# One of the two convolved chunks moves from TensorE to GpSimd, the squares of the head norms from GpSimd to ScalarE

## The reference

```python
def even_mixer(h, w_in, w_out, conv_w, conv_b, ln_g, ln_b, q_g, k_g, sinks):
    proj = h @ w_in
    a_val, a_gate, q, k, v = jnp.split(proj, cuts, axis=-1)      # 512, 512, 512, 128, 128 channels
    u = a_val * jax.nn.sigmoid(a_gate)
    u = lax.conv_general_dilated(u, conv_w[:, None, :], (1,), ((CONV_WIDTH - 1, 0),), ...,
                                 feature_group_count=CONV_CH) + conv_b     # 31 taps, one filter a channel
    u = jax.nn.silu(layer_norm(u, ln_g, ln_b))
    q = rms_norm_2(q.reshape(b, s, SWA_KV_HEADS, SWA_GROUP, HEAD_DIM), q_g)   # 8 heads of 64
    k = rms_norm_2(k.reshape(b, s, SWA_KV_HEADS, HEAD_DIM), k_g)              # 2 heads of 64
    o, _, _ = banded_attention(q, k, v, SWA_WINDOW - 1, sinks)                # causal, 128 positions back
    return jnp.concatenate([u, o.reshape(b, s, -1)], axis=-1) @ w_out
```

## Time and profile before

| | before |
|---|---|
| median of 3 runs | 1739.1 us (1738.5 to 1739.69) |
| the profiled execution | 1739.11 us |
| its span in the trace | 1737.3 us |
| PE busy | 96% |
| DVE busy | 70% |
| ACT busy | 54% |
| POOL busy | 29% |
| the even mixer, first input unit to last output unit | about 938 to 1077 us |

### The profile page before, as it was taken

How to read it: one execution, slowest core, us unless ns; L and a number is a source line. 1 busy time by engine, 2 the same in 40 slices (tenths; PEclk the granted TensorE clock), 3 DMA queues, 4 the chain that set the end, 5 groups by cost and what they waited for, 6 DMA issues and landing times. The chain is left out here.

```text
span 1737.3 us, 30201 instructions
## 1 busy us (share of the span) xinstructions
PE 1663.6 (96%) x10274; PEld 1452.1 (84%) x10274; DVE 1212.2 (70%) x2026; ACT 940.8 (54%) x1549; POOL 510.7 (29%) x492
## 2 busy tenths in 40 slices
PE   7896999999997999999999998999999999899999
PEld 6785899988876999888889867888888889678888
DVE  5776777756776777667765956777577765867763
ACT  5454566534553666456645655665376644456652
POOL 0040433310222434234421004443144411444430
PEclk9998999999998999999999998999999999999999
DMA  7330465654322566556665303656556655246662
GB/s 255 99 120 25 126 189 181 220 174 146 104 80 62 169 182 206 193 169 186 201 201 156 118 16 110 193 183 218 163 176 190 208 185 166 86 122 188 186 219 96
DMA packets 70494, 272.09 MB, mean 157 GB/s; under 512 B 7824, under 2 KB 8976, under 8 KB 70416
## 3 DMA queue, kind: packets, MB, share of 16 engines
q1 hardware_dynamic: 70416, 271.07, 49.6%
HBM read 269.99 MB, written 1.05 MB: 156 GB/s over the span
## 5 line engine op out<-in xcount | busy, mean ns | idle before, releaser
L828 DVE TENSOR_TENSOR wl<-raw,wh 128x1024 fp32r<-128x1024 f32 (+1 forms) x470 | 619.5, 1318 | 127.4 <-ACT wh L536 121.5
L536 ACT ACTIVATE wh<-raw 128x1024 fp32r<-128x1024 f32 (+1 forms) x470 | 525.9, 1119 | 218.5 <-PE gb L1275 115.9
L1271 PE MATMUL gb<-hx,wh 128*128 128x512 f32 x1512 | 543.9, 399 | 0.0
L1272 PE MATMUL gb<-hx,wl 128*128 128x256 f32 x1512 | 424.9, 281 | 0.0
L1271 PE MATMUL gb<-gux,wh 128*128 128x512 f32 x960 | 341.3, 395 | 0.0
L1271 PEld LDWEIGHTS gb<-hx,wh 128*128 128x128 f32 x1512 | 284.8, 188 | 59.2
L1258 PE MATMUL gb<-hx,wh 128*128 128x256 f32 x1008 | 298.6, 296 | 18.3 <-DVE hx L845 10.1
L1272 PEld LDWEIGHTS gb<-hx,wl 128*128 128x128 f32 x1512 | 286.4, 189 | 7.6
L1259 PE MATMUL gb<-hx,wh 128*128 128x256 f32 x1008 | 287.9, 286 | 0.0
L1260 PE MATMUL gb<-hx,wl 128*128 128x256 f32 x1008 | 287.4, 285 | 0.0
L1272 PE MATMUL gb<-gux,wl 128*128 128x256 f32 x960 | 268.5, 280 | 0.0
(11 more groups left out here) (213 smaller groups left out, 2051.7 us busy)
## 6 DMA issues: line engine op xcount, KB each, us to landing
raw<-in_wa SPq DMA_DIRECT2D x374, 512.0 KB, 3.6
raw<-in_wb SPq DMA_DIRECT2D x96, 704.0 KB, 4.2
x<-in_x SPq DMA_DIRECT2D x2, 512.0 KB, 6.1
out_x<-x SPq DMA_DIRECT2D x8, 128.0 KB, 3.1
row<-in_row SPq DMA_DIRECT2D x1, 836.0 KB, 11.4
tab<-in_bias SPq DMA_DIRECT2D x3, 256.0 KB, 4.4
con<-in_const SPq DMA_DIRECT2D x1, 544.0 KB, 8.5
tab<-in_bias SPq DMA_DIRECT2D x1, 512.0 KB, 5.4
```

The lines of the kernel that those rows point to most:

```text
L536: nc.scalar.activation(wh[:, slot, 0:nt * P], raw[:, slot, 0:nt * P], ACT.Copy).then_inc(s_hi, 1)
L828: nc.vector.tensor_tensor(wl[:, slot, 0:nt * P], raw[:, slot, 0:nt * P], wh[:, slot, 0:nt * P].bitcast(f32), ALU.subtract).then_inc(s_lo, 1)
L1271: nc.tensor.matmul(bank[:, :], a, both(k), start=start and k == 0, stop=False)
L1272: nc.tensor.matmul(bank[:, 0:SEQ], b, high(k), start=False, stop=False)
```

## The change

Three things, all in the even mixer:

- Chunk 3 is no longer convolved on PE. The table loses its "diag" 4 to 7 and "taps" 4 to 7 (ACT's 31 diagonals and PE's 31 products) and gains one entry, "pconv", at unit 7 behind the second "operand". On POOL it is a new function, `convolve`: 31 products of the shifted operand with one tap, broadcast along the row, and 30 additions into `yc(6)`, 61 `tensor_tensor` instructions of 128x256. The products rotate through three parts of `kkf`, so that the product of tap k is issued ahead of the addition of tap k-1. An instruction waits for all but the one just issued.
- "convolved" 1 on ACT waits for POOL instead of PE's taps and reads `yc(6)` instead of PSUM. Its place in ACT's queue is the same.
- The three squares of the head norms are an ACT instruction (Square) at the same places of the table.

```diff
-               "even": "sigmoids diagonals operands ...
+               "even": "pool_convolved sigmoids diagonals operands ...
...
-                      (5, "conv", 3), (6, "taps", 1), (6, "conv", 8), (7, "sig", 3), (7, "taps", 2), (7, "operand", 1),
-                      (7, "conv", 9), (8, "taps", 3), (8, "conv", 10), (8, "diag", 4), (9, "turn", 0), (9, "convolved", 0),
+                      (5, "conv", 3), (6, "taps", 1), (6, "conv", 8), (7, "sig", 3), (7, "taps", 2), (7, "operand", 1), (7, "pconv", 0),
+                      (7, "conv", 9), (8, "taps", 3), (8, "conv", 10), (9, "turn", 0), (9, "convolved", 0),
...
+            def convolve(m):
+                src, prods = operand[1], [kkf[:, k * SEQ:(k + 1) * SEQ] for k in range(3)]
...
+                def product(k):
+                    tap = PRM["ecw"] + 31 * 3 + k
+                    step(nc.gpsimd.tensor_tensor(yc(6) if k == 0 else prods[k % 3], src[:, k:k + SEQ],
+                                                 view(prm[:, tap:tap + 1], [[0, SEQ]]), ALU.mult))
+                pool.wait_ge(m["operands"], 2)
+                product(0)
+                product(1)
+                for k in range(2, 31):
+                    pool.wait_ge(s_pch, steps[0] - 1)
+                    product(k)
+                    pool.wait_ge(s_pch, steps[0] - 1)
+                    step(nc.gpsimd.tensor_tensor(yc(6), yc(6), prods[(k - 1) % 3], ALU.add))
+                pool.wait_ge(s_pch, steps[0])
+                nc.gpsimd.tensor_tensor(yc(6), yc(6), prods[0], ALU.add).then_inc(m["pool_convolved"], 1)
...
-                        if what == "sqr":
+                        if what == "sqr" and kind != "even":
                             square(M[n], n, g, qk_groups(kind, l)[g])
...
+                elif what == "sqr" and kind == "even":
+                    c, gains, _ = qk_groups(kind, l)[g]
+                    act.wait_ge(s_y, Y0[n] + c + len(gains))
+                    if g >= 1:
+                        act.wait_ge(m["qk_normed"], g)
+                    nc.scalar.activation(sq[:, 0:len(gains) * SEQ], yc(c, len(gains)), ACT.Square).then_inc(m["qk_squared"], 1)
...
-                    act.wait_ge(m["taps_multiplied"], 4 * g + 4)
-                    nc.scalar.activation(yc(2 * c), gb[3][:, 0:SEQ], ACT.Identity, bias=col("ecb", c)).then_inc(m["convolved"], 1)
+                    if g == 0:
+                        act.wait_ge(m["taps_multiplied"], 4)
+                    else:
+                        act.wait_ge(m["pool_convolved"], 1)
+                    nc.scalar.activation(yc(2 * c), gb[3][:, 0:SEQ] if g == 0 else yc(2 * c), ACT.Identity, bias=col("ecb", c)).then_inc(m["convolved"], 1)
```

More of the change, by code:

```diff
@@ L239, in build_program @@
                         "stats_log stats_rsd c_copied").split(),
-               "even": "sigmoids diagonals operands taps_multiplied convolved ln_operand ln_sum ln_log ln_rsd ln_out ln_sig".split(), "odd": ["mix_psum", "pooled"]}
+               "even": "pool_convolved sigmoids diagonals operands taps_multiplied convolved ln_operand ln_sum ln_log ln_rsd ln_out ln_sig".split(), "odd": ["mix_psum", "pooled"]}
         M = {n: {w: sem(f"{k}{l}_{w}") for w in NAMES + OWN[k]}
@@ L296, in build_program @@
                       (3, "conv", 1), (3, "diag", 2), (4, "conv", 2), (4, "diag", 3), (5, "sig", 2), (5, "taps", 0),
-                      (5, "conv", 3), (6, "taps", 1), (6, "conv", 8), (7, "sig", 3), (7, "taps", 2), (7, "operand", 1),
-                      (7, "conv", 9), (8, "taps", 3), (8, "conv", 10), (8, "diag", 4), (9, "turn", 0), (9, "convolved", 0),
-                      (9, "conv", 11), (9, "diag", 5), (10, "diag", 6), (11, "sqr", 0), (11, "diag", 7), (12, "sum", 0),
-                      (12, "norm", 0), (12, "sqr", 1), (12, "taps", 4), (13, "attn", 0), (13, "sum", 1), (13, "norm", 1),
-                      (13, "sqr", 2), (13, "taps", 5), (14, "attn", 1), (14, "sum", 2), (14, "norm", 2), (14, "attn", 2),
-                      (14, "taps", 6), (14, "attn", 3), (14, "taps", 7), (14, "attn", 4), (14, "convolved", 1),
+                      (5, "conv", 3), (6, "taps", 1), (6, "conv", 8), (7, "sig", 3), (7, "taps", 2), (7, "operand", 1), (7, "pconv", 0),
+                      (7, "conv", 9), (8, "taps", 3), (8, "conv", 10), (9, "turn", 0), (9, "convolved", 0),
+                      (9, "conv", 11), (11, "sqr", 0), (12, "sum", 0),
+                      (12, "norm", 0), (12, "sqr", 1), (13, "attn", 0), (13, "sum", 1), (13, "norm", 1),
+                      (13, "sqr", 2), (14, "attn", 1), (14, "sum", 2), (14, "norm", 2), (14, "attn", 2),
+                      (14, "attn", 3), (14, "attn", 4), (14, "convolved", 1),
                       (14, "attn", 5), (14, "ln", 0), (14, "ln", 1), (14, "attn", 6), (14, "ln", 2), (14, "attn", 7),
@@ L499, in pool_chunk, with step @@
                 nc.gpsimd.tensor_tensor(p, p, yc(12 + c), ALU.subtract).then_inc(m["pooled"], 1)
+            def convolve(m):
+                src, prods = operand[1], [kkf[:, k * SEQ:(k + 1) * SEQ] for k in range(3)]
+                def step(ins):
+                    steps[0] += 1
+                    ins.then_inc(s_pch, 1)
+                def product(k):
[12 more added lines that the diff above has]
+                nc.gpsimd.tensor_tensor(yc(6), yc(6), prods[0], ALU.add).then_inc(m["pool_convolved"], 1)
             for n, (kind, l) in enumerate(PHASES):
@@ L511, in _ @@
                             pool_chunk(M[n], g, n)
+                        elif what == "pconv":
+                            convolve(M[n])
                 else:
```

## The result

| | before | after |
|---|---|---|
| median of the runs on one chip (8 each) | 1738.42 us | 1744.28 us |
| lowest and highest | 1733.7 to 1739.69 us | 1740.52 to 1747.36 us |
| ratio after to before, 95% interval | | 1.0037 [1.0025, 1.0049] |
| the profiled execution, its span | 1739.11, 1737.3 us | 1743.34, 1741.4 us |

The changed kernel is slower by some 6 us, 0.37% with an interval clear of zero. It was forecast at 1747.5 us. The page of after, beside the earlier trace rows, says nothing of that: PE has 8.8 us less work, POOL 48 us more, DVE 15.5 us more although it does the same instructions.

A forecast was written before the change was run, and what follows sets the result against it. PE, 96% busy, bounds the whole kernel; at the change the path runs through DVE, POOL and PE's taps. On 1739.11 us, 8.8 + 2.0 - 2.4 = +8.4 us gave 1747.5 us, range 1737 to 1754 us (8 in 10).

The forecast's parts named there:

- (b) The loss of a tap: DVE's convolution of chunk 2: each instruction with two SBUF inputs loses 0.41 us while POOL is convolving.
- third rival: DVE beside POOL: each instruction loses a whole POOL instruction, 0.61 us, giving 1754 us; or POOL starves. Above 1751: 0.13.
- POOL starving: DVE wins each turn, POOL ends at 1030 to 1034, ACT waits: 1745 to 1749 us; shares 0.60 with turns.
- (b) The charge on L828: DVE up to the first head norm's end: five of these instructions charged 0.41 us each beside POOL.
- (b) The slack in front of step 0: Between first head norm and attention step 0's scores: 3.95 us absorbs part of 12.8 us, leaving +8.8 us.
- Even then PE is done: Ahead of attention step 0: with unit 13 at the lower clock, 5.8 us, PE still finishes at about 1009.3.
- (c) Steps 0 to 2: Attention steps 0 to 1 and 1 to 2: no taps to lose, 1.0 us each for sharing with POOL, +2.0 us.
- (c) The taps that leave PE: Attention steps 2 to 4: two steps fall from 5.07 and 4.67 to 3.65 us each, -2.4 us.
- (d) The squares: Three head-norm squares moved from POOL to ACT: taken as nothing, the later two up to 0.5 us each either way.
- (e) POOL's cover: At "convolved" 1: POOL done at about 1028, ACT asks at 1032.4, so covered with 4 us.
- The clock: PE at half clock, perhaps more of 996 to 1030: left out of the sum, else 1 to 3 us, upwards only.

The follow-up runs named there:

- e2: The changed kernel with one POOL product instead of the 61 convolution instructions, so chunk 3 is not convolved; 1732.2 us, ratio 0.9967 to the kernel before.
- e3: The changed kernel with PE's taps and ACT's diagonals of chunk 3 kept beside POOL's convolution; 1749.79 us, ratio 1.0061 to the kernel before.
- e5: The changed kernel with POOL's convolution held back until DVE's convolution of chunk 2 is done; 1750.95 us, ratio 1.0070 to the kernel before.
- e10: The changed kernel with 8, 12 and 3 products of constants put on PE in three of its gaps; 1742.18 us, ratio 1.0031 to the kernel before.
- e1: The kernel before with only the three head-norm squares moved to ACT, PE keeping chunk 3's taps; 1735.15 us, ratio 0.9987.
- e7: The changed kernel with chunk 3's 31 products on ACT and only 30 sums on POOL, begun behind DVE's convolution; 1739.44 us, ratio 1.0004 to before.
- e11: e7 with its last seven ACT products moved behind the second square, and 6 filler products on PE; 1735.37 us, ratio 0.9984 to the kernel before.
- e4: The changed kernel with 80 memsets of 128x512 and a small one on POOL behind its first product, chunk 3 not convolved; 1747.26 us, ratio 1.0051 to before.
- e12: The kernel before with only 6 products of constants on PE ahead of the last attention product; 1733.44 us, ratio 0.9977.
- e9: e1 with 6 products of constants on PE ahead of the last attention product; 1732.2 us, ratio 0.9972 to the kernel before.

## Why the prediction was right, and where not

The forecast was 1747.5 us, slower, by turns between DVE and POOL. The time is 1744.28, within the range, and e2, e3 and e5 show the mechanism. Several terms were mis-sized, mostly on the high side. Step by step:

**(b) The loss of a tap: right.** 0.41 us was taken from rows of other instructions in other layers, and the taps lost 0.41 us (0.82 against 0.406); over all 23 it is 0.39, since the first piece of eight took 6.00 us. The first head norm's two instructions took 1.70 us instead of 0.88, as taken. The loss was 0.41 us and not a whole POOL instruction of 0.61 or 0.72 us. The Trainium skill, in "SBUF — State Buffer", § Who interferes with whom, makes the shared port an exclusive lock that the later one waits for in full; the traces agree with the lock (L974 with two SBUF inputs is slowed, L1158 with one in PSUM is not) and not with that size of wait, so the first half of the third rival fell with it. Its other half, POOL starving until 1030 to 1034 and ACT waiting for it, fell as well: POOL's last sum ended at 50.43 local, which is 1027.7 on the clock of before, and ACT did not wait.

**(b) The charge on L828: mis-sized.** Each of the five L828 was charged 0.41 us too, 2.05 us in all. The first two of them in after took 1.24 and 1.22 us, against 1.22 in before, so they lost nothing. The next three took 1.41, 1.29 and 1.42, 4.12 us in all; in before they took 1.22, 1.73 and 1.22, 4.17 us, because there the middle one met the first square on POOL, which the change takes away. Where L865 began first it was POOL that waited (1.59 us for a product of 0.61); where POOL had begun, L865 lost up to 0.57 us (1.79 in e10). With these 2.05 us, with 0.5 us less in the first piece of taps and 0.2 less in the last sum (0.64 us for 0.43), unit 10 is late by 9.31 us and not 10.7, and the norm by 9.97 and not 12.8.

**(b) The slack in front of step 0: a little too large, and from the wrong row.** All 3.95 us between norm and scores were counted as free, and PE used 0.94 of them (scores 0.94 us behind the norm in after): 9.97 - 3.95 + 0.94 = 6.96. PE was at unit 13 still, at half clock, as the 1000 to 1003 stretch shows. "Even then PE is done", the prediction said of that case; it was done 0.94 us late. But what the step goes on with is the row maxima, and they are 7.0 us late whether the scores come 0.94 us behind the norm (after) or 0.06 (e10), because DVE must do another L865 first. Step 0 was forecast 1.8 us too late: 2.8 us too much for the norm, 0.94 too little behind it.

**(c) Steps 0 to 2: right.** +1.91 us for a charge of 2.0. From the row maxima of step 0 to those of step 2 it is 8.76 us in before and in e2 and 10.67 in after, and e10, at full clock, has 10.68: the whole difference is POOL's work.

**(c) The taps that leave PE: right in kind, too small.** Steps 2 to 3 and 3 to 4 fell from 5.07 and 4.67 us to 3.17 and 3.29, together -3.28 us where -2.4 was forecast. Both had been put at 3.65, which is 2.65 for a step without taps and 1.0 for turns. The charge was about right, and the 2.65 too large: in e2, without POOL's work, these two steps take 2.06 us each, so POOL's price is 1.1 and 1.2 us. It stands in DVE's `tensor_scalar` instructions, L1027, L1030 and L1061, and not in the short one with two tensor inputs (L1047, 0.15 us in both kernels). Two of them in step 3 of after, and the same two in e2:

```profile
1022.25 0.65 DVE L1030 TENSOR_SCALAR small<-small 128x2 f32<-128x2 f32 x1
...
1023.20 1.13 DVE L1061 TENSOR_SCALAR pr<-pr,small 128x256 f32<-128x256 f32 x2
```

```profile
1008.49 0.17 DVE L1023 TENSOR_SCALAR small<-small 128x2 f32<-128x2 f32 x1
...
1008.96 0.62 DVE L1054 TENSOR_SCALAR pr<-pr,small 128x256 f32<-128x256 f32 x2
```

**(d) The squares: a miss by themselves, open in the sum.** Taken as nothing; alone (e1) they are worth 2 to 4 us, 1.2 of them by the first square (1.96 us on POOL, 0.63 on ACT) and 1.9 by PE's clock behind the third. The reason given, that DVE and not the square is last at that place, does not hold for the kernel before: in e1 the first head norm ends 0.5 us later than in before, and step 0 still starts 1.2 us earlier, through PE. For after it seems to hold: e10 brought PE forward there by 0.85 us and gained nothing. How much of the gain is left in after was not tried: no run has POOL's convolution with the squares left on POOL, where in the table's order they would stand behind its 61 instructions.

**(e) POOL's cover: the sign right, the size not.** "Convolved" 1 did not wait. POOL's last sum ended at 50.43 local, where the forecast had 50.7 (1028 less 977.31), and ACT came at 52.32 instead of 55.1: 1.9 us of cover instead of 4. The number of POOL was right with wrong parts: a sum costs 0.72 us clear, not 0.61. With the mixer faster, the cover was nearly gone.

**The clock: left out, and it takes part.** "Upwards only, 1 to 3 us" was the remark. e10 gives 1 to 2 us. In after half clock is granted from about 997 to 1003.5, from 1010.5 to 1017.5 and from 1021 to 1031, each time behind a stretch in which PE had stood idle or nearly so. Only the last stretch costs time: there +5.64 us at "convolved" 1 turns into +6.66 at the first output unit, and into +4.63 in e10.

The medians split the result into three terms: squares -3.2 us (before to e1), taps off PE and diagonals off ACT -3.0 (e1 to e2), POOL's 60 instructions +12.1 (e2 to after). That they add up to the +5.9 between before and after is so by construction; their sizes are what is measured. The terms are not independent: the taps off PE are worth 5.5 us beside POOL's work (e3 to after).

## What to carry to other kernels

An idle POOL is not free room where DVE works on SBUF beside it: look for a place in the trace where the two already meet, take the loss per instruction from there, kind by kind, and multiply it by DVE's instructions in that stretch, not by POOL's. Look at the engine's idle stretches at the place of the change, not at its share on the page: ACT at 54% had no room for 13 us of products where 9.5 us of diagonals had stood (e7, e11). And before relieving an engine that is at 96%, look what its clock does in the gaps: here six products of constants in a 3.2 us gap gave 3.3 us locally, nearly as much as the best other part (3.9, e1).

## What the runs showed of the hardware that was not expected

- DVE and POOL take turns, but not evenly: a short tap loses 0.41 us at each turn and POOL's product and sum grow from 0.61 and 0.72 to 0.79 and 0.9 us, while a DVE instruction of 1024 columns loses 0 to 0.2 us in after and makes POOL wait up to 1.1 us (a sum of 1.80 us at the longest). Who began first matters: L865 lost 0.57 us in e10, where a sum of POOL had begun 0.02 us ahead of it.
- In after, DVE's `tensor_scalar` instructions, with one tensor input, lose too: 128x2 elements in 0.46 us instead of 0.23 (L1027) and in 0.53 to 0.65 instead of 0.17 (L1030), two of 128x256 in 1.13 instead of 0.62 (L1061). The row maxima, which read PSUM, keep their 0.41 us.
- POOL's writes alone leave DVE's taps at 0.406 us (e4), but a DVE `tensor_scalar` of 128x2 elements stood for 16.20 us, until the last of 80 memsets issued without a pause had ended. Why that instruction and not the taps was not settled; in after, where POOL's stream is of `tensor_tensor`, that instruction took 0.46 us and the next, L1030, 0.53 us, against 0.23 and 0.17 in before.
- PE's clock fell to 1.2 GHz behind an idle gap of 1.40 us in before (1.39 in e12), and not behind one of 1.14 us at the same place in e1 and e9. The gap alone does not decide it: one of 1.52 us later in before left the clock at 2.4 GHz. So gaps much shorter than those of 4 to 6 us can cost the clock, and which ones do has to be read from the trace.
